# Expert choice over 80 rows of 512 columns, with the long request's list joined from two halves

## The reference

```python
def _ec_moe(h, w_router, w_gate, w_up, w_down):
    t = b * s
    tok = h.reshape(t, d)
    aff = jax.nn.softmax((tok @ w_router).astype(jnp.float32), axis=-1)
    cap = max(1, CAPACITY_FACTOR * t // N_EXPERTS)      # 64 for prompt, 128 for sample
    gate, idx = lax.top_k(aff.T, cap)
    xe = tok[idx]
    hid = jax.nn.silu(jnp.einsum('ecd,edf->ecf', xe, w_gate)) * jnp.einsum('ecd,edf->ecf', xe, w_up)
    ye = jnp.einsum('ecf,efd->ecd', hid, w_down) * gate[..., None].astype(h.dtype)
    out = jnp.zeros_like(tok).at[idx.reshape(-1)].add(ye.reshape(-1, d))
```

## Time and profile before

| | |
|---|---|
| median of 3 runs | 3150.38 us |
| lowest and highest run | 3148.04 and 3151.98 us |
| profiled execution, its own time | 3152.26 us |
| its span, first to last instruction | 3150.6 us |
| mean granted clock of PE | 0.954 |
| PE busy | 2821.0 us, 90% of the span |
| DVE busy | 2168.8 us, 69% |
| ACT busy | 1536.0 us, 49% |
| POOL busy | 180.8 us, 6% |

### The profile page before, as it was taken

One profiled execution on the slowest core, in us unless ns is written; L12 is line 12 of the kernel. 1 busy time (PEld: TensorE's weight loads), 2 busy tenths in 40 slices (PEclk: granted clock), 3 DMA queues, 4 the chain that ended last, 5 costly groups with the idle time before them and its releaser, 6 DMA issues. The chain is left out here.

```text
span 3150.6 us, 50850 instructions
## 1 busy us (share of the span) xinstructions
PE 2821.0 (90%) x17878; PEld 2415.1 (77%) x17878; DVE 2168.8 (69%) x4112; ACT 1536.0 (49%) x2882; POOL 180.8 (6%) x180
## 2 busy tenths in 40 slices
PE   5999487799997893699999999999999999999993
PEld 4988254366665782599999999999999999999992
DVE  3566465556665447777877887887787788788774
ACT  3443244444444231455555555555565555655552
POOL 0000010011010000000000000000000000000001
PEclk8999799899999996799999999999999999999996
DMA  6221300112212340768777876886777777678664
GB/s 246 68 71 46 104 21 35 58 51 88 96 47 96 139 155 32 241 218 250 245 224 245 250 231 225 250 246 220 248 244 224 241 246 239 223 243 250 224 196 170
DMA packets 359719, 547.41 MB, mean 174 GB/s; under 512 B 14784, under 2 KB 287936, under 8 KB 359616
## 3 DMA queue, kind: packets, MB, share of 16 engines
q1 hardware_dynamic: 350720, 514.59, 49.2%
q0 software_dynamic: 8896, 31.46, 4.3%
HBM read 493.51 MB, written 52.49 MB: 173 GB/s over the span
## 5 line engine op out<-in xcount | busy, mean ns | idle before, releaser
L2470 PE MATMUL banks<-rowsT_parts,weights_high 128*128 128x384 f32 x4096 | 1184.0, 361 | 12.1 <-DVE hidden_parts L2401 7.0
L2471 PE MATMUL banks<-rowsT_parts,weights_low 128*128 128x192 f32 x4096 | 1026.3, 251 | 0.0
L2470 PEld LDWEIGHTS banks<-rowsT_parts,weights_high 128*128 128x128 f32 x4096 | 770.1, 188 | 21.3 <-DVE hidden_parts L2401 9.8
L2471 PEld LDWEIGHTS banks<-rowsT_parts,weights_low 128*128 128x128 f32 x4096 | 783.7, 191 | 1.4
L2481 PE MATMUL banks<-weights_high,hidden_parts 128*128 128x512 f32 x1536 | 435.4, 392 | 0.0
L2388 DVE TENSOR_TENSOR gate_up_sums<-banks,gate_up_sums 128x192 f32<-128x192 f32 x512 | 181.1, 354 | 328.4 <-ACT gate_up_sums L2306 328.4
L2306 ACT ACTIVATE gate_up_sums<-banks 128x192 f32<-128x192 f32 x512 | 165.0, 322 | 453.1 <-PE banks L2471 449.2
L2481 PEld LDWEIGHTS banks<-weights_high,hidden_parts 128*128 128x128 f32 x1536 | 283.5, 188 | 69.9
L2481 PE MATMUL banks<-weights_low,hidden_parts 128*128 128x512 f32 (+1 forms) x1024 | 319.6, 393 | 0.0
L2338 DVE TENSOR_TENSOR weights_low<-slab_up,weights_high 128x1024 fp32r<-128x1024 f32 x256 | 311.6, 1217 | 0.0
L2338 DVE TENSOR_TENSOR weights_low<-slab_down,weights_high 128x1024 fp32r<-128x1024 f32 x256 | 311.2, 1216 | 0.0
(11 more groups left out here) (277 smaller groups left out, 3734.2 us busy)
## 6 DMA issues: line engine op xcount, KB each, us to landing
slab_gate<-w_gate SPq DMA_DIRECT2D x128, 1024.0 KB, 5.4
slab_up<-w_up SPq DMA_DIRECT2D x128, 1024.0 KB, 7.3
slab_down<-w_down SPq DMA_DIRECT2D x128, 1024.0 KB, 4.8
arena_attend<-w_ada SPq DMA_DIRECT2D x8, 2048.0 KB, 7.9
arena_attend<-ssd_tiles SPq DMA_DIRECT2D x12, 992.0 KB, 8.1
arena_inputs<-w_ada SPq DMA_DIRECT2D x4, 2048.0 KB, 12.7
ssd_tiles<-arena_inputs SPq DMA_DIRECT2D x24, 256.0 KB, 2.0
mixed<-arena_attend SPq DMA_DIRECT2D x12, 512.0 KB, 2.6
```

Source lines behind the costliest of these rows:

```text
L2470: nc.tensor.matmul(out[:, 0:2 * CT], w_hi[:, u, block], x[:, k, :], start=k == 0, stop=False)
L2471: mm = nc.tensor.matmul(out[:, 0:CT], w_lo[:, u, block], x[:, k, 0:CT], start=False, stop=k == KD - 1)
```

## The change

The table of affinities has 80 rows of 512 columns. Prompt stays in rows 0 to 15. Sample's tokens 0 to 511 are in rows 32 to 47, its tokens 512 to 1023 in rows 64 to 79. The sixteen rounds run over the 80 rows and give each half its 128 greatest in falling order. The list of the first half (`best[low]`) and that of the second half read backwards (`mirror`) are then laid against each other, and of each pair the greater is kept, with its place: of two ordered lists of 128 this gives the 128 greatest of both together, in another order. The place is picked with arithmetic: `first` is 1 where the first half's value is at least the mirror's, and the place is `(place - mirror_place) * first + mirror_place`.

DVE's program of the output stage is written out tile by tile (`tile_by_tile`), since the row of the affinities' copy now hangs on the tile's number. The other engines keep `tile_pipeline`.

```diff
+def tile_by_tile(phases):
+
+    least, most = min(ahead for ahead, _ in phases), max(ahead for ahead, _ in phases)
+    for t in range(-most, NT - least):
+        for ahead, step in phases:
+            if 0 <= t + ahead < NT:
+                step(t + ahead, (t + ahead) % 2, int(t + ahead >= TILES[1][0]))
...
-    aff = core.aff = A.at(A_AFF, 1024)
+    aff = A.at(A_AFF, 512)
...
-            nc.vector.memset(aff[0:48, :], -1.0)
+            nc.vector.memset(aff[0:80, :], -1.0)
...
-                nc.vector.tensor_copy(aff[32 * r:32 * r + NE, bass.ds((g - TILES[r][0]) * P, P)],
-                                      core.ps[5][0:NE, 0:P]).then_inc(aff_done, 1)
+                half, at = divmod((g - TILES[r][0]) * P, 512)
+                row = 32 * (r + half)
+                nc.vector.tensor_copy(aff[row:row + NE, at:at + P], core.ps[5][0:NE, 0:P]).then_inc(aff_done, 1)
...
-            tile_pipeline(dve, [(-2, top_logit), (-1, residual), (-2, softmax), (-1, norm), (-1, shift),
+            tile_by_tile([(-2, top_logit), (-1, residual), (-2, softmax), (-1, norm), (-1, shift),
                                 (-2, affinities), (1, low)])
...
-    left = [A.at(A_AFF, 1024)[0:48, :], A.at(0, 1024)[0:48, :]]
-    best = A.at(1024, CAP[1])[0:48, :]
-    place = A.at(1152, CAP[1])[0:48, :]
-    places = core.small("places", [48, CAP[1]], U32)
+    left = [A.at(A_AFF, 512)[0:80, :], A.at(0, 512)[0:80, :]]
+    best, place, mirror, mirror_place, first, gap = (A.at(1024 + 128 * i, CAP[1])[0:80, :] for i in range(6))
+    places = core.small("places", [80, CAP[1]], U32)
     ranked, turned = sem("choice_order"), sem("choice_turned")
+    low, high = slice(32, 32 + NE), slice(64, 64 + NE)
...
             nc.vector.tensor_copy(place[0:32], places[0:32, :])
-            order.link(nc.vector.tensor_scalar(place[32:48], places[32:48, :], float(T_OF[0]), None, ALU.add))
+            nc.vector.tensor_copy(mirror[low], best[high, ::-1])
+            nc.vector.tensor_scalar(mirror_place[low], places[high, ::-1], float(T_OF[0] + 512), None, ALU.add)
+            order.link(nc.vector.tensor_scalar(place[low], places[low, :], float(T_OF[0]), None, ALU.add))
+            nc.vector.tensor_tensor(first[low], best[low], mirror[low], ALU.is_ge)
+            order.link(nc.vector.tensor_tensor(gap[low], place[low], mirror_place[low], ALU.subtract))
+            order.link(nc.vector.tensor_tensor(gap[low], gap[low], first[low], ALU.mult))
+            nc.vector.tensor_tensor(best[low], best[low], mirror[low], ALU.max)
+            order.link(nc.vector.tensor_tensor(place[low], gap[low], mirror_place[low], ALU.add))
...
-            nc.tensor.transpose(core.ps[0][:, 0:48], place, core.ident[0:48, 0:48])
-            nc.tensor.transpose(core.ps[0][:, 64:112], best, core.ident[0:48, 0:48]).then_inc(turned, 1)
+            nc.tensor.transpose(core.ps[0][:, 0:48], place[0:48], core.ident[0:48, 0:48])
+            nc.tensor.transpose(core.ps[0][:, 64:112], best[0:48], core.ident[0:48, 0:48]).then_inc(turned, 1)
```

## The result

| | before | after |
|---|---|---|
| median (20 runs each, same chips) | 3159.29 us | 3136.32 us |
| lowest and highest | 3148.04, 3171.16 | 3132.04, 3150.78 |
| ratio after / before | | 0.9941, 95% interval 0.9927 to 0.9954 |
| profiled execution, own time and span | 3152.26, 3150.6 | 3135.97, 3134.3 |

The kernel became faster, by 0.59%; 0.75% was forecast (a ratio of 0.9925), and the median of 3136.32 us lies above the range of 3121 to 3133 us.

A forecast was written before the change was run, and what follows sets the result against it. The prediction took DVE, working alone in the choice, as the bound there: -25.5 us for the rounds and +1.8 for the longer end make -23.7, so 3150.4 becomes 3126.7 us, range 3121 to 3133.

The forecast's parts named there:

- What bounds the stretch: In the choice DVE works alone for 59.75 of 62 us; a microsecond off its chain should be one off the kernel.
- Rival (b): After the choice, PE comes out of the shorter pause at its 2.4 GHz level, 2.8 us less: 3123.9; chance 3%.
- The lists in half the columns: Sixteen rounds of the choice: three instructions each lose 532 ns at 512 columns, 25.5 us in all; 80 rows cost nothing.
- rival (a): The choice's columns are cheaper than the reduction's: 11.4 us gained, 3139.0, chance 5%; the opposite, halved in full: 3123.2, 2%.
- The joining: End of the choice: two more front instructions and five TENSOR_TENSORs of 16x128 add 1.8 us.
- The mirrored reads: Two backward reads at the choice's end: taken at 0.21 us each; by the page's worst figure 0.37 us more together.
- The output stage: Shorter memset, another row for affinities and DVE's written-out tiles: nothing gained or lost, since DVE has air in every tile.
- What follows the choice: Experts stage: nothing was loaded under the choice, so the whole of the experts moves forward as it is.
- Rival (d): Output stage: DVE's written-out tiles are fetched late, 8.0 us a tile, 32 us in all: 3158.7; chance 1%.
- The range: Whole kernel: tail bounds 3126.5 to 3127.1, widened by the runs' spread and some 3 us for experts: 3121 to 3133.

The follow-up runs named there:

- e4: Kernel before with DVE's output stage written out tile by tile, the choice left over 48 rows of 1024 columns; ratio to before 1.0001.
- e2: Changed kernel with 103 semaphore counts that nobody waits for, added to DVE's stream in the output stage; ratio to before 0.9924.
- e3: Changed kernel with DVE's loop over tiles kept in the output stage instead of written out; ratio to before 0.9926.
- e7: Changed kernel with 39 semaphore counts that nobody waits for, added to DVE's stream in the output stage; ratio to before 0.9919.
- e9: Changed kernel with DVE's loop over experts 2 to 14 written out; ratio to before 0.9923.
- e6: Changed kernel with 14 semaphore counts that nobody waits for, added to DVE's stream in the output stage; ratio to before 1.0030.
- e8: e3 with 20 semaphore counts that nobody waits for, added to DVE's stream in the output stage; ratio to before 0.9925, thirteen experts 1461.73 us.
- e11: e3 with 21 semaphore counts that nobody waits for, added to DVE's stream in the output stage; thirteen experts 1466.65 us, one execution.

## Why the prediction was wrong, point by point

- **What bounds the stretch:** right. Nothing lay beside the choice, and its 23.75 us moved the first load of weights one for one. Rival (b) fell: PE came out of the shorter pause at the same level, with a mean clock of 0.94 up to the third gather in both kernels.
- **The lists in half the columns:** right. 532 ns less for each instruction was forecast; MAX8 lost 529 ns (1220 to 691), and sixteen rounds lost 60.19 - 34.72 = 25.47 us where 25.5 was said. The reduction of the earlier trace rows was the right neighbour; rival (a) fell on both sides. That 80 rows cost what 48 do is right to 0.13 us.
- **The joining:** 1.8 us was said, 1.71 measured. The mirrored reads took 0.22 and 0.21 us, as if read forwards. For a step back by one word, the Trainium skill's figures for small steps (Vector Engine (DVE) Microarchitecture Reference, section Measured stream behaviour on trn2) do not apply here.
- **The output stage:** right in itself. The written-out tiles were free there (e4), and in their midst DVE still waited for ACT before it split the next tile's input, for 5.64 us where it had been 5.33.
- **What follows the choice: this step failed.** The prediction said that "the whole of the experts moves forward as it is", and of the longer code: "It costs more instructions to fetch, perhaps 80 [...] I put this at nothing". It was 26 instructions in all by the built program, 27 by the trace. Nothing waited for them where they stand, but they shifted the loop over the experts, two stages later, to a place where each of its turns has code fetched again, and that loop lost 0.52 us at each of thirteen turns: 6.75 us. With that term the sum for the ratio is -23.7 + 6.8 = -16.9 us, where the ratio gives -18.6, a gain between 14.5 and 23.1 by its interval. The term alone takes the forecast median out of the range: 3126.7 + 6.8 is 3133.5. Rival (d) had the right kind of thing, code that arrives late, at the wrong place (the tiles, not the next loop), and so it asked for 10.6 us a tile before it would matter.
- **The rule that I read past:** the Trainium skill, Runtime: NRT & Kernel Launch, section Instruction fetch mechanics, says that a taken branch whose target lies outside the pages at hand has to wait for a fetch. The prediction looked at the loop that the change removes, where DVE had air. It did not ask what the rule makes of the loops behind it. The trace agrees with the rule in kind. The page speaks of blocks of 16 KiB, 256 instructions, and of two at hand. As an estimate from that page, a loop of 286 would touch three blocks instead of two at about 30 of 256 places; the theory of the experiments, with pieces of 128, gives 30 places too. The band of places in which the loop paid is between 15 and 44 instructions wide (from 2366 to 2380, and neither 2360 nor 2405), so both fit. The transfers here are of 8.2 KB and not 16 KiB, and no run tells whether the band comes back every 128 instructions or every 256.
- **The range:** it was laid around three runs of the kernel before that all happened to be of the earlier group, and the wider spread could not be seen in them. By its own terms (3127.1, 1.6 for the spread, 3 for the experts) its upper end would be 3131.7 and not 3133. The earlier group of the changed kernel alone, at 3134.67, lies above it either way.

With the loop where it fits, the forecast holds: e2, e3, e7 and e9 have ratios of 0.9924, 0.9926, 0.9919 and 0.9923 for 0.9925 forecast, each with an interval of some 0.0025 to either side. Their thirteen experts are 6.6 to 8.1 us shorter than in the changed kernel as given; the ratios point the same way, though their intervals still touch its own. Among the four no difference can be told. e3 is the one that I would keep, with an eye on q14, since its program is the shortest; e9 is the one that doesn't hang on where the loop begins.

What stays open: how much code DVE holds at once, by what order it is replaced, and so why a turn costs five transfers in the band and none outside it. Open too is how a transfer makes the instruction late. In e6 one transfer on q14 runs from 1967.66 to 1968.04 us, and the instruction that stands starts at 1969.61. In the changed kernel the five transfers of the turn at 1950.14 us begin 2.8, 3.2, 8.9, 17.9 and 67.0 us after it, and none runs during the stand before 1965.10. The link between transfers and stand rests on their coming and going together in fourteen traces, and on the fixed place 2112. The cost ran from 0.17 us an expert (2366) over 0.52 (2367) to 2.4 (2380), by which instruction stood at that place, and at 2380 by the clock that fell as well.

## What to carry to other kernels

Lengthening an engine's program can slow a loop that was never touched: whenever instructions are added or taken away ahead of a long loop, compare the count of instruction transfers in the page and inside one turn of the loop, and if they rose, shift the loop by a few fillers in idle time, or write it out. Where one engine works alone in a stage, durations from the nearest rows can be summed; here the sum came within a tenth of a microsecond. And a median of three runs is no base for a range on a kernel whose executions fall into two groups: forecast the ratio.

## What was not expected of the hardware

- A loop of 286 instructions on DVE cost nothing when its end stood at 2340 to 2360, 2405 or 2469 of the stream, and up to 2.4 us a turn at 2366 to 2380, with 60 transfers of 8.2 KB more in the whole kernel.
- The late code cost more than its own wait: after stands of 1.75 us in e6 the granted clock fell to 0.50 for 3.4 us, eight times, and these experts took 1.5 us longer than their neighbours.
- One instruction more (e8 to e11) raised thirteen experts from 1461.7 to 1466.7 us.
- The stall shows in the trace as "issue", or as a wait for a forerunner that was already done (0.61 us instead of 0.25), never as a DMA.
